# A hybrid SSD / gated-delta / product-key layer on one core: input projections in parts of two, three and three tiles instead of two halves

## The chip, the cores and the metric

One core of a Trainium2 chip runs the whole layer in one launch. The metric is the device time of one execution in microseconds (us), the median of several runs. All data is float32.

## The reference, cut to what matters

```python
def reference(x, ...):                      # x: (1, 1024, 1024)
    for l in range(1):
        x = x + hybrid_mixer(rmsnorm(x, norm_mix_w[l]), w_in[l], ...)
        x = x + peer_ffn(rmsnorm(x, norm_ffn_w[l]), ...)
    return rmsnorm(x, norm_final_w)

def hybrid_mixer(hn, w_in, ...):
    proj = hn @ w_in                        # 1024 -> 3600 columns: z, xBC, dt, qkv, gate, beta, alpha
    xbc = silu(causal_dwconv(proj[xBC], ssd_conv_w) + ssd_conv_b)     # 4 taps along the frames
    qkv = silu(causal_dwconv(proj[qkv], gdn_conv_w))
    ...                                     # SSD scan and gated delta rule, causal from frame to frame
    return concat(y_ssd, y_gdn) @ w_out

def peer_ffn(hn, w_q, sub_keys, u_tab, v_tab):   # per token: 8 heads x 16 experts of 16384
    ...                                          # scores, two top-16, idx and gates (128 per token)
    act = gelu(einsum('td,tkd->tk', hb, u_tab[ib]))
    return einsum('tk,tkd->td', gb * act, v_tab[ib])
```

The input projection is `hn @ w_in`. A convolution over four frames follows it on 20 of its column blocks. The expert part reads 128 rows of `u_tab` and 128 rows of `v_tab` for each token, 4 KB a row.

## The kernel before, in words

The sequence of 1024 frames is cut into 8 tiles of 128. The projection's columns are cut into 29 **units** of 128 columns (the last has 16): units 0 to 19 go through the convolution, 20 to 27 are gates, 28 is the small one of the heads. A unit of some tiles is 8 matmuls that accumulate (one for each 128 rows of `w_in`; the trace shows each as two instructions), then the convolution on VectorE, SiLU on ScalarE, transposes on TensorE, a copy on ScalarE, and stores to scratch tensors in HBM (`tok_scr`, `zgs_scr` by frame, `ch_scr` by channel).

The program has these stages, in order:

- `front_stage` normalises and turns the x tiles (`rms`, `scale_x`, `turn_x`, `weigh`) and projects the **first half**, tiles 0 to 3, so each matmul has 512 columns. Tiles 4 to 7 are normalised between the units (`norm_after`) and kept in SBUF, in slots of the ring that the gathers use later. The order on TensorE is `project(u)`, `turn(u - 1)`, and where `norm_after(u)` names a tile, `turn_x`.
- `tile_stage` first loads constants, then runs `body(0, None)`: the mixer and the product-key selection (`steps`) of tile 0, with the folding of `w_q` and the keys between its pieces. This is "tile 0" below.
- Then come ten **gather stages** e = 0 to 9. Stage e runs `steps` of tile e + 1, the U gathers and dots of tile e (VectorE: 128 gathers of 128 rows, 512 KB each), and the V gathers and sums of tile e - 1 (TensorE: 128 gathers, in pairs). `steps` calls `share()` between its pieces. Each engine then does the items of a list (`SEQUENCES`) that fall to that share, in the list's order: U is a U gather's dot, V a V gather's sum. Every engine works in its own program order, so an item whose input is late holds up all that stands behind it there.
- The **second half** of the projection, tiles 4 to 7 in units of 512 columns, is in stage e = 0: items B (matmuls), Q (copy out of PSUM), K (convolution), Z (SiLU), D (transposes), Y (copy). `first_sequence` places them by shares: D and Y of the unit before, then B, Q, K of this one, then Z. There is one buffer for the copy out of PSUM (`b_pre`) and one for the sums (`b_mixed`). SP loads the weights of unit u + 2 behind the stores of unit u.

The gathers go through a ring of slots of 512 KB, in turn. POOL issues a gather when the slot's last user is done. In stage 0 the ring has `FEW` = 6 slots, because the other 5 hold the turned tiles and a unit's weights; from stage 1 on it has all 11. The weights of a unit are read from `w_in` as it lies, 128 columns wide, so in rows of 512 bytes.

## Time and profile before

| | |
|---|---|
| median of 3 runs | 3464.66 us (3463.91 to 3464.87) |
| the profiled execution | 3463.27 us |
| its span, first to last instruction | 3461.5 us |
| so around the span | 1.8 us |
| TensorE busy, mean granted clock | 2560.1 us (74%), 0.903 |
| VectorE busy | 2069.9 us (60%) |
| ScalarE busy | 469.0 us (14%) |
| GpSimd busy (it issues the gathers) | 1983.2 us (57%) |
| moved by DMA | 1167.46 MB, 337 GB/s over the span |

Busy shares are averages over stages with different limits, so the table only says that no engine is full all the time. What limits a stage has to be read stage by stage. A granted clock of 1.0 is TensorE's level of 2.4 GHz, 0.5 that of 1.2 GHz; a value between is a mixture over the stretch.

### The profile page before, as it was taken

How to read it: one execution, taken by the hardware profiler on the slowest of the kernel's cores; microseconds unless marked ns; L12 is line 12 of the kernel's file. 1: busy time of each engine (PE TensorE's matmuls, PEld its weight loads, DVE VectorE, ACT ScalarE, POOL GpSimd, SP SyncE). 2: the span in 40 equal slices, each digit the busy share in tenths (PEclk: the TensorE clock that was granted, in tenths of full speed). 3: DMA queues.
4: the chain of work that ended last, by engine and by line, in shares of the span. 5: the costliest groups of instructions: out<-in, count | busy, mean ns of one | idle time of the engine just before them, and what ended most of it. 6: DMA issues, size and time to landing. Idle time of an engine off the chain costs nothing.

```text
span 3461.5 us, 26069 instructions
## 1 busy us (share of the span) xinstructions
PE 2560.1 (74%) x8616; PEld 960.6 (28%) x8616; DVE 2069.9 (60%) x4643; ACT 469.0 (14%) x1001; POOL 1983.2 (57%) x2099
## 2 busy tenths in 40 slices
PE   7996636698578757875787587857885888566698
PEld 3446324443233113311421142113211421111111
DVE  3304365558886758685777577767776776544400
ACT  3314112233211001001010100010001100000000
POOL 1110011123477767776777677767776777777775
PEclk9998867799799989998999899989998989888999
DMA  4444045467899999999999999999999999999998
GB/s 121 131 122 140 0 147 164 146 224 248 318 406 409 409 407 396 410 409 407 397 409 409 406 398 409 409 403 400 409 409 403 402 409 409 410 410 410 409 402 355
DMA packets 395350, 1167.46 MB, mean 337 GB/s; under 512 B 40720, under 2 KB 120368, under 8 KB 395216
## 3 DMA queue, kind: packets, MB, share of 16 engines
q0 software_dynamic: 298112, 1082.93, 79.8%
q1 hardware_dynamic: 94048, 78.52, 7.2%
q10 hardware_dynamic: 3056, 4.35, 0.3%
q8 instruction: 69, 1.13, 0.1%
q14 instruction: 65, 0.53, 0.0%
HBM read 1143.57 MB, written 22.09 MB: 337 GB/s over the span
## 4 chain that ended last, share of the span: by engine, by line
POOL 33%; PE 18%; DMA 17%; issue 12%; DVE 9%; ACT 2%; SPq 0%; DVEq 0%; POOLq 0%; ACTq 0%
POOL ring L819 33%; DMA ring<-in_peer_v_dram,picks_T 9%; DMA ring<-in_peer_u_dram,picks 7%; PE y_psum L849 6%; PE y_psum L894 3%; DVE ring L1269 2%; PE tile_psum L1047 2%; DVE arena L1502 1%; DVE arena L1506 1%; PE tile_psum L970 1%; PE tile_psum L988 1%; PE tile_psum L989 1%; DVE final_row L1262 1%; PE tile_psum L1026 1%; DVE arena L1509 1%
## 5 line engine op out<-in xcount | busy, mean ns | idle before, releaser
L894 PE MATMUL y_psum<-ring,spread 128*32 128x512 f32 x4096 | 1370.4, 646 | 504.9 <-DMA ring<-in_peer_v_dram,picks_T 503.5
L1269 DVE CUSTOM_DVE_ANT_0 ring<-ring,h_psum 128x1024 f32<-128x1024 f32 x1024 | 1235.7, 1218 | 700.7 <-DMA ring<-in_peer_u_dram,picks 684.5
L819 POOL DMA_INDIRECT ring<-in_peer_u_dram,picks x1024 | 976.0, 953 | 876.5 <-DVE dots L1269 358.4
L819 POOL DMA_INDIRECT ring<-in_peer_v_dram,picks_T x1024 | 970.8, 948 | 360.3 <-issue 284.8
L894 PEld LDWEIGHTS y_psum<-ring,spread 128*32 128x32 f32 x4096 | 265.3, 113 | 1511.0 <-DMA ring<-in_peer_v_dram,picks_T 919.4
L1047 PE MATMUL tile_psum<-w_q,arena 128*128 128x512 f32 x512 | 224.1, 597 | 2.2 <-ACT arena L1214 2.2
L370 PE MATMUL proj<-hn_first,w_blk 128*128 128x512 f32 x448 | 201.5, 605 | 1.3 <-DVE hn_first L474 1.3
L1117 ACT COPY spread<-zero 128x8 f32<-128x8 f32 (+1 forms) x104 | 21.6, 207 | 1080.0 <-PE y_psum L894 1080.0
L1047 PEld LDWEIGHTS tile_psum<-w_q,arena 128*128 128x128 f32 x512 | 97.3, 191 | 127.6 <-issue 124.8
L1026 PE MATMUL tile_psum<-w_out,arena 128*128 128x512 f32 x256 | 118.0, 605 | 0.0
L1297 DVE SCALAR_TENSOR_TENSOR res<-res,stat_e,final_row 128x1024 f32<-128x1024 f32 x8 | 10.3, 1283 | 177.3 <-ACT stat_e L1134 177.3
L370 PEld LDWEIGHTS proj<-hn_first,w_blk 128*128 128x128 f32 x448 | 85.3, 195 | 100.0 <-issue 98.3
L849 PE MATMUL y_psum<-ring,res 128*128 128x512 f32 x224 | 108.1, 639 | 5.4 <-DMA res<-in_w_in_dram 5.4
L849 PE MATMUL y_psum<-ring 128*128 128x512 f32 x224 | 108.7, 642 | 3.1 <-DMA ring<-in_w_in_dram 3.1
L1259 DVE TENSOR_SCALAR final_row<-b_pre,taps 128x512 f32<-128x512 f32 x20 | 9.7, 486 | 149.8 <-ACT b_pre L1082 149.8
L988 PE MATMUL tile_psum<-arena 128*128 128x128 f32 x320 | 71.0, 306 | 31.4 <-ACT arena L1172 21.6
L346 POOL DMA_DIRECT2D tok_scr<-frames x18 | 13.6, 755 | 125.5 <-ACT frames L441 125.5
L1269 DVE DVE_READ_ACCUMULATOR2_ANT dots<- 128x1 f32 x1024 | 84.2, 82 | 0.0
L989 PE MATMUL tile_psum<-arena 128*128 128x128 f32 x384 | 76.1, 292 | 5.4 <-ACT arena L1172 5.4
L970 PE MATMUL tile_psum<-arena 128*128 128x128 f32 x384 | 58.4, 298 | 27.4 <-DVE arena L1423 27.4
L970 PEld LDWEIGHTS tile_psum<-arena 128*128 128x128 f32 x384 | 49.8, 202 | 59.9 <-issue 59.5
L1026 PEld LDWEIGHTS tile_psum<-w_out,arena 128*128 128x128 f32 x256 | 46.7, 191 | 68.4 <-issue 64.2
(234 smaller groups left out, 2239.8 us busy)
## 6 DMA issues: line engine op xcount, KB each, us to landing
ring<-in_peer_u_dram,picks POOLq DMA_INDIRECT x1024, 8.4
ring<-in_peer_v_dram,picks_T POOLq DMA_INDIRECT x1024, 9.8
w_blk<-in_w_in_dram SPq DMA_DIRECT2D x28, 512.0 KB, 3.8
ring<-in_w_q_T_dram SPq DMA_DIRECT2D x16, 512.0 KB, 3.7
ring<-in_w_in_dram SPq DMA_DIRECT2D x14, 512.0 KB, 7.8
res<-in_w_in_dram SPq DMA_DIRECT2D x14, 512.0 KB, 7.8
arena<-tok_scr SPq DMA_DIRECT2D x8, 768.0 KB, 9.1
tok_scr<-frames POOLq DMA_DIRECT2D x18, 256.0 KB, 2.9
```

The source lines that it names most:

```text
L370: last = nc.tensor.matmul(proj[u % 2][0:width(u)], w, hn[0][:, k], start=(k == 0), stop=(k == KD - 1))
L819: pool.indirect_dma_start(ring[:, j], None, tables[kind], bass.IndirectOffsetOnAxis(ap=at, axis=0)).then_inc(filled[j], 16)
L849: last = nc.tensor.matmul(y_ps[0:unit_width(n), n % 2], w, hn[:, k], start=(k == 0), stop=(k == KD - 1))
L894: last = nc.tensor.matmul(y_ps[quad * STEPS:(quad + 1) * STEPS, half], lines[:, quad, at:at + STEPS], ring[:, j, half * BANK:(half + 1) * ...
L970: last = nc.tensor.matmul(heads(1)[:, h], M_T[:, n % 2, h], X[:, h], start=True, stop=True)
L988: nc.tensor.matmul(heads(2)[:, h], Y[:, h], MX[:, h], start=True, stop=True)
L989: last = nc.tensor.matmul(heads(0)[:, h], MX[:, h], Y[:, h], start=True, stop=True)
L1026: last = nc.tensor.matmul(bank[:, 1 + half], mixT[:, k], w_out[:, k, half * BANK:(half + 1) * BANK], start=(k == 0), stop=(k == KD - 1))
L1047: last = nc.tensor.matmul(bank[:, SCORE_BANKS[b]], h_T[:, k], w_q[:, k, b * BANK:(b + 1) * BANK], start=(k == 0), stop=(k == KD - 1))
L1262: stt(out=b_mixed, in0=b_pre[:, tap:tap + HALF], scalar=taps[:, tap, n:n + 1], in1=b_mixed, op0=ALU.mult, op1=ALU.add).then_inc(s["b_tap"], 1)
L1269: nc.vector.tensor_tensor_reduce(out=ring[:, j], in0=ring[:, j], in1=h_ps[:], scale=1.0, scalar=0.0, op0=ALU.mult, op1=ALU.add, accum_out= ...
L1502: tt(chosen, rank_ps[:, None, None, :].broadcast_to(full), top_rank[:, hs, :, None].broadcast_to(full), ALU.is_equal).then_inc(s["chosen_r ...
```

## The change

The projections now come in three parts:

- **Tiles 0 and 1** in `front_stage`, 256 columns a matmul. Six tiles (2 to 7) are normalised between the units, one in every third. The convolution reads the matmul's result straight from PSUM, so `pre` and its copy go. Four weight buffers stand in place of two. The turned tiles 5 to 7 are written to a new scratch tensor `hn_scr`. The constants of `tile_stage` are loaded here too.
- **Tiles 2 to 4** in gather stage 0, 384 columns a matmul. The items are placed by gathers (`with_units`): B and Q, K and Z two gathers later, D and Y three more gathers later. There are two buffers for the sums, the convolution reads PSUM, its first tap is taken on ScalarE as it copies, and SP loads the next weights ahead of the stores.
- **Tiles 5 to 7** in gather stages 1 to 3, 9, 10 and 10 units, 384 columns each, in the PSUM bank that the transposes use too (`b_bank`), with one weight buffer and one sums buffer.

The ring has `FEW` = 7 slots in stages 0 to 3, and 11 from stage 4 on. The weights are laid out by units on the host (`w_units`), so that a partition reads 4 KB in one piece. They are read three times instead of twice.

The diff, cut to its core:

```diff
-HALF = SEQ // 2
-HALF_TILES = HALF // P
+FIRST_TILES, PART_TILES = 2, 3
+PARTS = 1 + (TILES - FIRST_TILES) // PART_TILES
+FIRST, PART = FIRST_TILES * P, PART_TILES * P
+LATE = (PARTS - 1) * UNITS
+UNITS_OF = {0: (0, UNITS)} | {1 + n: (UNITS + UNITS * n // 3, UNITS + UNITS * (n + 1) // 3) for n in range(3)}
-FEW = 6
+FEW = 7
+def with_units(seq, ends, e):
+    first, to = UNITS_OF[e]
+    total = len([item for item in seq if item[0] in "UV"])
+    begin, gap = (1, 2) if e == 0 else (16, 5)
+    points = []
+    for n in range(first, to):
+        at = begin + (total - begin - 3 * gap) * (n - first) // (to - first)
+        points += [(at, n, "BQ"), (at + gap, n, "KZ"), (at + 2 * gap + (e == 0), n, "DY")]
...
+FEW_STAGES = max(UNITS_OF) + 1
 for e, items in enumerate(GATHERS):
+    if e == FEW_STAGES:
+        CYCLE, count = [*range(FEW, SLOTS), *((count + j) % FEW for j in range(FEW))], 0
     for n, item in enumerate(items):
-        j = n % FEW if e == 0 else CYCLE[later % SLOTS]
-        later += e > 0
+        j = count % FEW if e < FEW_STAGES else CYCLE[count % SLOTS]
...
             def load_w(u):
-                if u >= 2:
-                    sp.wait_ge(proj_done, u - 1)
-                sp.dma_start(w_blk[:, u % 2], w_in[:, :, col:col + P]).then_inc(w_loaded[u % 2], 16)
+                if u >= W_BUFS:
+                    sp.wait_ge(proj_done, u - W_BUFS + 1)
+                    sp.dma_start(w_blk[:, u % W_BUFS], A["w_units"][u]).then_inc(w_loaded[u % W_BUFS], 16)
...
             def norm_after(u):
-            return HALF_TILES + u // 4 if u % 4 == 1 and u < 4 * HALF_TILES else None
+            return FIRST_TILES + u // 3 if u % 3 == 1 and u < 3 * (TILES - FIRST_TILES) else None
...
             def conv(u):
-                dve.wait_ge(pre_done, u + 1)
+                dve.wait_ge(proj_done, u + 1)
+                nc.vector.tensor_copy(halo[:, u], proj[u % 2][:, FIRST:])
...
                 if e == 1:
+                    all_stored(UNITS)
...
+                for n in range(*UNITS_OF.get(e, (0, 0))):
+                    if n < UNITS - 2 or n >= UNITS - 1:
+                        load_unit(n + 2 if n < UNITS - 2 else n + 1)
+                    tile, u = FIRST_TILES + n // UNITS * PART_TILES, n % UNITS
+                    if by_channel(u):
+                        sp.wait_ge(s["b_silu"], n + 1)
+                        sp.dma_start(ch_scr[u, :, tile * P:tile * P + PART], unit_sums(n)).then_inc(b_ch_stored[n % 2], 16)
+                    if by_token(u):
+                        sp.wait_ge(s["b_framed"], LATE_TURNED[n] + 1)
+                        sp.dma_start(part["frames_out"](tile, PART_TILES, u), ...)
...
-                    if e == 1 and j >= FEW and turn_of(item, e) == 1:
-                        pool.wait_ge(s["b_proj"], UNITS)
+                    if j >= FEW and turn_of(item, e) == 1:
+                        pool.wait_ge(s["b_proj"], LATE)
...
                 if kind == "Q":
+                        nc.scalar.copy(unit_bank(n)[:, 0:HALO], halo[:, u]).then_inc(s["b_pre"], 1)
+                        nc.scalar.copy(halo[:, u], unit_bank(n)[:, PART:PART + HALO])
+                        nc.scalar.activation(unit_sums(n), unit_bank(n)[:, 0:PART], ACT.Copy, scale=taps[:, 0, u:u + 1]).then_inc(s["b_pre"], 1)
```

On TensorE, at the head of the front stage (`proj` is a unit's result, `turned` its transposes, `x_turned` an x tile), before and after:

```order
L358 MATMUL x_turned<-ident_f,x_in 128x128 x32
L370 MATMUL proj<-hn_first,w_blk 128x512 x16
L381 MATMUL turned<-ident_f,conv_sum 128x128 x4
L358 MATMUL x_turned<-ident_f,x_in 128x128 x8
L370 MATMUL proj<-hn_first,w_blk 128x512 x8
```

```order
L400 MATMUL x_turned<-ident,x_in 128x128 x16
L408 MATMUL proj<-hn_first,w_blk 128x256 x16
L419 MATMUL turned<-ident,conv_sum 128x128 x2
L400 MATMUL x_turned<-ident,x_in 128x128 x8
L408 MATMUL proj<-hn_first,w_blk 128x256 x8
```

Two x tiles stand ahead of the first unit instead of four, and each unit is half as wide; a turned x tile still stands behind the second unit.

On TensorE in gather stage 0, around the scores of tile 1 (`y_psum<-ring` is a unit's matmuls, `b_turned` or `b_bank` its transposes, `tile_psum` a piece of `steps`), before and after:

```order
L857 MATMUL b_turned<-ident_m,final_row 128x128 x4
L849 MATMUL y_psum<-ring 128x512 x8
L857 MATMUL b_turned<-ident_m,final_row 128x128 x4
L849 MATMUL y_psum<-ring,res 128x512 x8
L951 MATMUL tile_psum<-arena 128x64 x8
L956 MATMUL tile_psum<-ident_m,arena 128x128 x4
L962 MATMUL tile_psum<-S_ssd,arena 128x256 x2
L857 MATMUL b_turned<-ident_m,final_row 128x128 x4
```

```order
L901 MATMUL y_psum<-ring,res 128x384 x8
L909 MATMUL b_bank<-ident,final_row 128x128 x3
L1003 MATMUL tile_psum<-arena 128x64 x8
L901 MATMUL y_psum<-ring 128x384 x8
L909 MATMUL b_bank<-ident,final_row 128x128 x3
L1008 MATMUL tile_psum<-ident,arena 128x128 x4
L1014 MATMUL tile_psum<-S_ssd,arena 128x256 x2
L1022 MATMUL tile_psum<-arena 128x128 x4
```

The transposes now stand behind the next unit's matmuls, not ahead of them, and the units are spread by gathers.

On TensorE at the start of gather stage 1 (`y_psum<-ring,spread` is a pair of V gathers), before and after:

```order
L866 MATMUL y_psum<-y,ident_m 128x512 x2
L916 MATMUL tile_psum<-arena 128x128 x2
L894 MATMUL y_psum<-ring,spread 32x512 x4
L920 MATMUL tile_psum<-rate,upper 128x12
L921 MATMUL tile_psum<-rate,ones 128x12
```

```order
L918 MATMUL y_psum<-y,ident 128x512 x2
L901 MATMUL b_bank<-ring 128x384 x8
L968 MATMUL tile_psum<-arena 128x128 x2
L946 MATMUL y_psum<-ring,spread 32x512 x4
L972 MATMUL tile_psum<-rate,upper 128x12
L973 MATMUL tile_psum<-rate,upper 128x12
```

A unit's matmuls now stand between the V gathers and the pieces of `steps` here, and at 28 more places in stages 1 to 3.

## Rows read from the trace of the kernel before

**Rows 1.** Busy times by stage: front, tile 0, gather stages 0, 1 and 2.

```profile
core 0: us, PE busy (x) PEld busy (x) DVE busy (x) ACT busy (x) POOL busy (x), PEclk, DMA share, GB/s
25.40:260.50 235.10, 222.26 (x604) 103.88 (x604) 62.01 (x88) 71.43 (x125) 26.46 (x37) 0.98 0.40 121
260.50:457.00 196.50, 113.05 (x627) 84.59 (x628) 93.60 (x309) 55.78 (x168) 0.00 (x0) 0.80 0.19 62
457.00:919.20 462.20, 339.86 (x949) 177.83 (x947) 287.76 (x636) 142.74 (x194) 123.57 (x132) 0.84 0.63 205
919.20:1267.00 347.80, 255.83 (x907) 88.93 (x907) 247.19 (x565) 29.98 (x74) 253.43 (x266) 0.91 1.03 407
1267.00:1605.00 338.00, 252.59 (x892) 85.89 (x893) 241.10 (x554) 27.79 (x70) 241.87 (x255) 0.91 1.02 405
```

**Rows 2.** Timeline of TensorE, front stage (start, us, instruction): tile, two units, last transposes.

```profile
45.02 1.81 PE L358 MATMUL x_turned<-ident_f,x_in 128*128 128x128 f32 x8 [2.14 <-DVE x_in L469]
...
232.05 7.03 PE L370 MATMUL proj<-hn_first,w_blk 128*128 128x512 f32 x16
...
239.35 7.03 PE L370 MATMUL proj<-hn_first,w_blk 128*128 128x512 f32 x16
...
253.72 1.20 PE L381 MATMUL turned<-ident_f,conv_sum 128*128 128x128 f32 x8
```

**Rows 3.** Timeline of TensorE in tile 0: four instructions of 256 columns.

```profile
301.97 1.03 PE L962 MATMUL tile_psum<-S_ssd,arena 128*128 128x256 f32 x4
```

**Rows 4.** Timeline of ScalarE and GpSimd, front stage: SiLU, norm's end, bias load.

```profile
39.29 0.72 ACT L453 ACTIVATE conv_sum<-conv_sum,conv_bias 128x512 f32<-128x512 f32 x1 [1.49 <-DVE conv_sum L484]
...
43.98 0.20 ACT L413 ACTIVATE rstd<-log_ms 128x1 f32<-128x1 f32 x1
...
21.24 0.88 POOL L337 DMA_DIRECT2D conv_bias<-in_ssd_conv_b_dram  x1
```

**Rows 5.** Groups by form, VectorE: multiply-add of 512 and 128 columns, scaling a tile.

```profile
L1262 DVE SCALAR_TENSOR_TENSOR final_row<-b_pre,taps,final_row 128x512 f32<-128x512 f32 x60 | 45.1, 751 | 2.1
L1362 DVE SCALAR_TENSOR_TENSOR arena<-tile_psum,logs,floor 128x128 f32<-128x128 f32 x96 | 25.6, 342 | 9.4 <-PE tile_psum L907 9.4
L469 DVE TENSOR_SCALAR x_in<-x_in,rstd 128x1024 f32<-128x1024 f32 x8 | 6.1, 756 | 34.0 <-ACT rstd L413 28.8 <-DMA ident_f<-in_c_ident_dram 5.3
```

**Rows 6.** Timeline of SP at `tile_stage`'s start: first constant, first load of tile 0.

```profile
260.55 0.34 SPq L750 DMA_DIRECT2D ident_m<-in_c_ident_dram  x1
...
264.33 0.52 SPq L760 DMA_DIRECT2D arena<-tok_scr  x1
```

**Rows 7.** Chain of waits over 457 to 925 us: shares by line, two pieces.

```profile
by line: PE y_psum L849 43.0%; DVE final_row L1262 6.5%; PE tile_psum L1047 5.9%; DMA res<-in_w_in_dram 4.9%; issue 4.6%; DMA ring<-in_w_in_dram 3.9%; PE b_turned L857 3.6%; PE tile_psum L1026 2.9%; PE tile_psum L988 2.2%; PE tile_psum L989
...
459.07 18.43 DMA ring<-in_w_in_dram
...
843.68 11.88 DMA res<-in_w_in_dram
```

**Rows 8.** Waits over gather stage 0: who, for whom, total us, times, longest.

```profile
DVE final_row L1259 <- ACT b_pre L1082: 149.8, 20, 12.3
```

**Rows 9.** DMA queues of the page: packets, MB, share of 16 engines.

```profile
q1 hardware_dynamic: 94048, 78.52, 7.2%
```

**Rows 10.** The gathers' issues (L819) over 919 to 1945 us.

```profile
  DVE dots L1269: 34.7, 31
  PE y_psum L894: 34.1, 37
...
DMA to landing us min/median/max: 5.4/8.7/16.5
```

**Rows 11.** Stretches of 20 us in stage 2 (columns of rows 1); a V pair.

```profile
1347.00:1367.00 20.00, 15.74 (x90) 9.57 (x90) 15.57 (x27) 2.88 (x7) 15.31 (x16) 0.91 1.03 408
1367.00:1387.00 20.00, 17.96 (x115) 11.18 (x115) 13.26 (x24) 2.56 (x6) 13.81 (x15) 1.00 0.99 373
...
1079.17 1.91 PE L894 MATMUL y_psum<-ring,spread 128*32 128x512 f32 x8
```

More of the change, by code:

```diff
@@ L441, in frame @@
                     nc.scalar.copy(frames[:, u % 2, :, 0:width(u)], turned[u % 2][:, :, 0:width(u)]).then_inc(frames_done, 1)
[L443 removed]
+            for i in range(FIRST_TILES):
                 rms(i)
@@ L521, with tile_stage @@
 ARENA = 11024
-def tile_stage(nc, A, half, ch_scr, tok_scr, zgs_scr, out, w_out, w_q, ring, w_late_loaded):
+def tile_stage(nc, A, part, fixed, ch_scr, tok_scr, zgs_scr, hn_scr, out, w_out, w_q, ring, w_late_loaded, consts_loaded):
     ctx, sb, ps, sem = scope(nc)
@@ L562, in tile_stage @@
         res = sb("res", [P, D])
[L563 removed]
         final_row = sb("final_row", [P, D])
[L565 to L568 removed]
+        b_late = sb("b_late", [P, PART])
+        b_w = [ring[:, SLOTS - 1], res[:]]
+        hn, taps, conv_bias, halo = (part[n] for n in ("hn", "taps", "bias", "halo"))
         picks_T = [sb(f"picks_T{j}", [P, P], U32) for j in range(2)]
@@ L920, in steps @@
                 nc.tensor.matmul(bank[:, 0, 0:HEADS], upper[:], rate[:], start=True, stop=True)
-                nc.tensor.matmul(bank[:, 0, HEADS:2 * HEADS], ones[:], rate[:], start=True, stop=True).then_inc(s["cums_ready"], 1)
+                nc.tensor.matmul(bank[:, 0, HEADS:2 * HEADS], ones, rate[:], start=True, stop=True).then_inc(s["cums_ready"], 1)
                 share()
@@ L1102, in do @@
+                if kind == "Y" and by_token(n % UNITS):
+                    act.wait_ge(s["b_turned"], LATE_TURNED[n] + 1)
+                    if by_channel(n % UNITS):
+                        act.wait_ge(b_ch_stored[n % 2], 16 * len([k for k in range(n % 2, n + 1, 2) if by_channel(k % UNITS)]))
+                    nc.scalar.copy(unit_frames(n)[:, :, 0:unit_width(n)], b_turned[:, :, 0:unit_width(n)]).then_inc(s["b_framed"], 1)
                 if kind == "G":
```

422 lines of the change are left out of this document (213 added, 209 removed).

## The prediction

> **What bounds the kernel now.** I read the busy times by stage first, because an average over this kernel hides four different limits [rows 1]. In the front stage TensorE is busy 222 of 235 us while the DMA share is 0.40, so the width and number of matmuls set it. Tile 0 takes 196.5 us and is a chain of small steps. Gather stage 0 takes 462.2 us with TensorE at 340, VectorE at 288 and DMA at 0.63: no engine and no queue is full, so a chain through several engines sets it. From stage 1 on the DMA share is 1.02 to 1.03 at 405 to 407 GB/s, with TensorE busy 253 and VectorE 241 of 338 us. Those stages are bound by the gathers' bytes, 256 gathers in 338 us, 1.32 us each.
>
> The chain of waits over stage 0 says what its chain is made of [rows 7]: 43.0% of 468 us, about 200, is the units' matmuls, 8.8% or 41 us is waiting for unit weights (18.4 of it at the start, 11.9 and 10.9 near the end), 6.5% or 30 us the convolution's multiply-adds, 3.6% or 17 us the transposes. The whole width of a unit is on the path. The waits agree: VectorE stood 149.8 us at the head of 20 convolutions, 7.5 us each, for the copy that follows the unit's matmuls [rows 8], with the dots and the steps of tile 1 queued behind it.
>
> So the change takes work out of two stages where it is on the path, and puts a third of it into three stages where DMA is full and TensorE has some 85 us free.
>
> **The front stage.** A unit with its transposes takes 7.30 us (239.35 - 232.05) [rows 2]. With 256 columns both parts halve: 3.65 us. Four instructions of 256 columns take 1.03 us [rows 3], so 16 of them take no more than 4.1 us; I take 3.65 and keep 4.3 as the upper bound of a unit.
>
> Six tiles are now normalised between units. Such a tile is ready after this sequence: convolution of the unit before, about 1.9 us (three multiply-adds of 256 columns at 0.48, between the 0.34 of 128 and the 0.75 of 512 columns [rows 5], and 0.5 for the first tap and the halo, an estimate from the same rows), SiLU 0.45 (half of 0.72, plus some), 4.2 us from SiLU's end to the end of `rstd` (40.0 to 44.2) [rows 4], and 0.76 for the scaling [rows 5]. That is 7.3 us, of which the next unit covers 3.65. With the hand-overs TensorE then idles about 4 us (2.1 before) [rows 2], and turns the tile in 1.8 us. Three units with one tile: 3 x 3.65 + 1.8 + 4 = 16.8 us, and six of these are 101 us. The first convolution cannot start before the bias lands, issued at 21.2 [rows 4], so at about 26. Then 26 + 101 + 10 x 3.65 + the tail of 6.8 us (253.7 to 260.55) [rows 2, 6] = 170 us against 260.5: **-90 us**. With units of 4.3 us it is -71; if the idle time shrinks by half it is -102. The weights are loaded four units ahead, and half of the old DMA share was unused, so the loads, the constants that move in and the 1.6 MB for `hn_scr` are hidden. If they weren't, each unit would wait for 0.5 MB, and that is the -71 case again.
>
> **Setup.** Eight constant loads on SP stand ahead of the first load of tile 0, 260.55 to 264.33 [rows 6]. They go: **-4 us**. Tile 0 stays.
>
> **Gather stage 0.** Matmuls: 200 us x 384/512 = 150, **-50**. Transposes: three for four, **-4**. Weight waits: the two late ones of 11.9 and 10.9 us come from a load that stands behind the unit's stores on SP; now it stands ahead of them, **-22**. The start (18.4 us) stays, since it shares the queues with the loads of tile 1. The copy and convolution: VectorE now does two dots before it turns to K, the first tap is on ScalarE, and TensorE does the next unit before D. Of the 7.5 us wait for each convolution about 2.6 are filled and 1.7 go with the narrower unit (counted already); the multiply-adds fall from 0.75 to about 0.62. What is left on the path I estimate at 1 us less for each of 20 units, **-20**. Sum **-96**, so 366 us. The bounds are -50 (the matmuls alone) and -130 (all of the convolution and transposes hidden). TensorE's own sum, 340 - 54 = 286 us, excludes more. The seventh ring slot gives nothing, since the gathers don't set this stage.
>
> **Gather stages 1 to 3.** Nine or ten units each. Bytes: 9.67 x 0.524 = 5.1 MB of weights, at 405 GB/s 12.5 us. The stores: about 9.3 x 384 + 2.7 x 128 = 3,900 packets. The 94,048 packets of SP's queue took 7.2% of 3461 us [rows 9], 2.65 ns each over all 16 engines, so 10 us. Together 23 us a stage on a full queue, with nothing to hide it. One 1.6 MB load of the turned tiles adds 4 us once.
>
> TensorE: 16 instructions of 384 columns and three transposes, 5.5 us a unit, 53 us a stage on top of 253. That fits in 361 us on average, but not evenly: between 1367 and 1387 us TensorE was busy 18 of 20 us and the gathers' rate fell to 373 GB/s [rows 11]. The ring is 7 slots for 11 there. At 1.32 us each, 11 slots give a gather 14.5 us from its issue until its slot is free, 7 give 9.2. It needs 5.4 us to land at best (8.7 in the median, in a longer queue [rows 10]) and 1.9 us for a V pair [rows 11], 7.3 in all. About 2 us are left, where now POOL hardly waits for a slot (69 us in three stages) [rows 10]. A V pair that finds a unit of 5.1 us ahead of it uses more than that. I take 1.2 us lost for each unit, **12 us** a stage; nothing is the lower bound, all of TensorE's 53 us the upper. So a stage takes 35 us more, **+105** for three, between +54 (half of the 23 hidden behind the present gaps, and the start) and +228.
>
> **The sum.** 3463.3 (the profiled execution; the median of the runs is 3464.7, 1.4 more) - 90 - 4 - 96 + 4 + 105 = **3382 us**.
>
> **Rivals.**
> *The late units nearly free.* The ring of 7 is enough and the stores slip between gathers: +54 for +105, 3331 us. For it: 2 us of slack for each gather, and TensorE idle for a quarter of the stage. Against it: the DMA share is above 1.0, so bytes can't be free.
> *The late units cost their whole width: slower.* In stages 1 to 3 each unit blocks the V pairs, the seven slots fill, POOL stops and the queue runs dry, so a unit costs its 5.5 us of TensorE beside its bytes: 76 us a stage, +228, 3505 us. It decides against the change from 62 us a stage on, where three stages eat up 186. For it: stage 0, where just so 43% of the path is units; the stretch at 1367 us. Against it: most stretches of stage 2 kept 408 GB/s at 15 to 20 us of TensorE work.
> *Stage 0 shrinks by its matmuls alone,* since the steps of tile 1 are the chain and fill what the convolutions leave: -50 for -96, 3428 us. For it: tile 0 alone takes 196 us for such a chain, and 128 dots come on top.
> *Narrow matmuls don't shrink as their width,* since a weight load stands before each. The four instructions of 256 columns took 1.03 us [rows 3], 0.26 each where the half of the present ones is 0.21: at most 29 x 16 x 0.05 = 23 us lost in the front, 3405 us. Against it: the 0.26 holds the last one's drain. The Trainium skill (TensorE: Matmul & The Clock Gate, The mechanism) says that a weight load overlaps a running matmul only when their row groups differ, and gives a load of 128 columns 0.107 us, which would make it an estimated 50 us and 3432. By that rule 512 columns would show it too, and the trace disagrees: 7.03 us for 16, which leaves nothing between them [rows 2].
>
> **How the numbers follow.** A difference under 0.2% (7 us) can't be told from no change here. Chances: the forecast's case 0.47, late units nearly free 0.20, stage 0 by matmuls alone 0.12, narrow matmuls 0.02, late units at their whole width 0.15, and 0.04 for a sum of these that lands within 7 us. So faster 0.81, same 0.04, slower 0.15. The range of 8 in 10 reaches from 3315 (late units nearly free, and a little more from stage 0) to 3475 (stage 0 by its matmuls alone and stages 1 to 3 at 50 us more each, or those at 65 by themselves), leaving out the slower case's far half.
>
> **What would show it.** The start of tile 0's loads near 170 us; units of 3.65 us in the front with gaps of about 4 us ahead of each turned tile; stage 0 (first gather to the last dots) near 366 us, with no wait over 5 us for unit weights after its start; stages 1 to 3 near 375 us with a DMA share still close to 1.0, and from stage 4 on 338 to 340 as now. If stages 1 to 3 show POOL waiting for slots for more than 50 us each at a DMA share under 0.95, the ring's price was taken too low. If stage 0 is above 410 us, its chain wasn't the units'. Either would make the prediction wrong.

## The result, and the profile after

The changed kernel takes 3431.0 us in the median of four runs (3426.8 to 3437.1), beside 3464.8 (3463.9 to 3465.2) for the kernel before. The ratio is 0.9905, 95% interval 0.9891 to 0.9919: 34 us less, a gain clear of the 0.2% that counts, and inside the forecast range, where the forecast was 81 us less. The profiled execution is the slowest of the four, 3437.1 us with a span of 3435.3, so the trace has 26 us to explain and not 34. All ratios are of undisturbed executions; one of the kernel before, beside some of the experiments, took 5267.7 us and is left out.

Busy times by stage of the changed kernel: front, tile 0, gather stages 0 to 4. From stage 1 on a stage is cut here from the last U dot of one stage to the last of the next.

```profile
core 0: us, PE busy (x) PEld busy (x) DVE busy (x) ACT busy (x) POOL busy (x), PEclk, DMA share, GB/s
25.00:175.00 150.00, 119.48 (x540) 100.76 (x538) 51.42 (x112) 55.72 (x99) 23.73 (x36) 0.89 0.51 169
178.80:368.80 190.00, 112.76 (x627) 84.56 (x628) 93.38 (x308) 55.67 (x168) 0.00 (x0) 0.81 0.17 60
368.80:731.80 363.00, 262.39 (x922) 159.88 (x920) 269.38 (x615) 137.66 (x212) 123.95 (x131) 0.86 0.76 260
731.80:1118.30 386.50, 296.75 (x1027) 117.20 (x1027) 256.99 (x582) 64.69 (x128) 236.28 (x251) 0.89 0.97 364
1118.30:1510.30 392.00, 304.43 (x1084) 118.01 (x1084) 260.71 (x586) 72.81 (x142) 242.86 (x257) 0.92 0.98 372
1510.30:1897.90 387.60, 302.67 (x1084) 117.06 (x1084) 245.22 (x561) 63.11 (x114) 243.82 (x256) 0.93 0.97 370
1897.90:2239.70 341.80, 251.94 (x894) 87.42 (x894) 242.68 (x557) 29.01 (x72) 244.70 (x258) 0.92 1.02 405
```

Cut at the same points, the kernel before has 329.2, 340.2, 339.2 and 340.2 us in stages 1 to 4, the first two of them these:

```profile
918.60:1247.80 329.20, 243.05 (x862) 85.08 (x862) 241.21 (x557) 26.48 (x67) 240.31 (x253) 0.91 1.03 408
1247.80:1588.00 340.20, 253.37 (x894) 86.12 (x894) 242.94 (x558) 29.02 (x72) 244.41 (x258) 0.91 1.02 405
```

Stages 1 to 3 pay 57.3, 51.8 and 48.4 us more, 157.5 together. From the end of stage 3 on the two profiles differ by 3 us in all.

The other mark is the cast of the picks, which ends a tile and releases the gathers of its stage. Timeline of VectorE, the casts ahead of and behind stage 0, first before, then after:

```profile
456.95 0.22 DVE L1301 CAST picks<-arena 128x128 uint32<-128x128 f32 x1
914.97 0.22 DVE L1301 CAST picks<-arena 128x128 uint32<-128x128 f32 x1
```

```profile
368.80 0.22 DVE L1351 CAST picks<-arena 128x128 uint32<-128x128 f32 x1
728.14 0.22 DVE L1351 CAST picks<-arena 128x128 uint32<-128x128 f32 x1
```

The first cast comes 88.2 us earlier. Stage 0, cast to cast, falls from 458.0 to 359.3 us, by 98.7. So -88.2 - 98.7 + 157.5 + 3 = -26 us, the difference of the two profiled executions.

Front stage, timeline of TensorE with the transposes of a normalised tile, and of SP with the first load of tile 0:

```profile
100.20 3.62 PE L408 MATMUL proj<-hn_first,w_blk 128*128 128x256 f32 x16
...
107.85 1.97 PE L400 MATMUL x_turned<-ident,x_in 128*128 128x128 f32 x8 [3.81 <-DVE x_in L499]
109.61 4.12 PE L408 MATMUL proj<-hn_first,w_blk 128*128 128x256 f32 x16
```

```profile
178.85 0.33 SPq L797 DMA_DIRECT2D arena<-tok_scr  x1
```

The unit behind a turned tile takes 4.12 us here, and up to 5.71, where the others take 3.62. TensorE idles before each turned tile, and the granted clock is lower in the unit behind it. Windows over one unit each, behind the fifth and the sixth turned tile, then one with no tile ahead:

```profile
109.61:113.73 4.12, 4.12 (x19) 3.54 (x19) 1.43 (x2) 0.51 (x1) 0.00 (x0) 0.88 0.02 6
126.87:132.58 5.71, 5.71 (x19) 4.63 (x19) 1.43 (x2) 0.51 (x1) 0.00 (x0) 0.63 0.01 1
136.31:139.93 3.62, 3.62 (x20) 3.16 (x19) 2.00 (x5) 0.88 (x2) 0.71 (x1) 1.00 0.78 283
```

Stage 0, the waits: who, for whom, in all, times, longest; then the chain of waits over the stage, shares by line.

```profile
DVE final_row L1312 <- ACT final_row L1144: 67.0, 14, 9.4
...
PE y_psum L901 <- DMA ring<-in_w_units_dram: 24.4, 3, 19.8
...
PE y_psum L901 <- DMA res<-in_w_units_dram: 5.8, 4, 3.5
```

```profile
by line: PE y_psum L901 23.4%; DVE ring L1319 21.4%; PE tile_psum L1099 7.5%; DVE final_row L1312 5.7%; DMA ring<-in_w_units_dram 5.3%; PE tile_psum L1078 4.6%; DVE arena L1559 2.8%; issue 2.0%; DVE arena L1552 1.9%; DVE arena L1556 1.9%; D
```

The units' matmuls were 43.0% of the chain [rows 7] and are 23.4%; the dots (L1319), not among its first ten lines before, are 21.4%. The convolution's wait of 149.8 us [rows 8] is 67.0. TensorE idles 30 us for unit weights, 19.8 of it in the first wait. That is more than before. The waits of TensorE for unit weights in the old stage 0:

```profile
PE y_psum L849 <- DMA res<-in_w_in_dram: 5.4, 2, 3.5
PE y_psum L849 <- DMA ring<-in_w_in_dram: 3.1, 3, 1.4
```

Stages 1 to 3, the gathers' issues on GpSimd: what ended POOL's idle time (us, times), and the time from issue to landing.

```profile
  PE y_psum L946: 202.3, 126
  issue: 170.9, 556
  DVE dots L1319: 70.1, 81
...
DMA to landing us min/median/max: 4.2/6.4/11.3
```

POOL waits 272 us for a free slot in three stages, where it waited 69 [rows 10]. The landing is shorter than before, 6.4 for 8.7 us. (Both traces give the landing of only some nine in ten of these gathers.) That doesn't look like a queue with more bytes to carry; it looks like one with less in it.

### The profile page after: what moved, and what is told of

It is laid out like the page before. It is cut to its first block, busy times and chain, and to the rows that moved or that the text cites. A ratio compares the mean times of both kernels' runs of the same rounds, so it can differ in the third digit from the quotient of the medians.

```text
span 3435.3 us, 27404 instructions
## 1 busy us (share of the span) xinstructions
PE 2539.3 (74%) x9080; PEld 1040.8 (30%) x9080; DVE 2073.3 (60%) x4704; ACT 561.3 (16%) x1160; POOL 1975.4 (58%) x2097
## 4 chain that ended last, share of the span: by engine, by line
POOL 24%; DMA 24%; PE 22%; DVE 13%; issue 10%; ACT 2%; SPq 0%; DVEq 0%; ACTq 0%; POOLq 0%
POOL ring L869 24%; DMA ring<-in_peer_v_dram,picks_T 14%; DMA ring<-in_peer_u_dram,picks 9%; PE y_psum L946 7%; DVE ring L1319 4%; PE b_bank L901 3%; PE y_psum L901 2%; PE tile_psum L1099 2%; PE tile_psum L1078 2%; DVE arena L1552 1%; DVE arena L1556 1%; PE tile_psum L1040 1%; DVE arena L1559 1%; PE tile_psum L1041 1%; PE tile_psum L1022 1%
## 5 line engine op out<-in xcount | busy, mean ns | idle before, releaser
L1319 DVE CUSTOM_DVE_ANT_0 ring<-ring,h_psum 128x1024 f32<-128x1024 f32 x1024 | 1236.3, 1218 | 809.2 <-DMA ring<-in_peer_u_dram,picks 795.1
L901 PE MATMUL b_bank<-ring 128*128 128x384 f32 (+1 forms) x464 | 156.0, 490 | 0.0
L1347 DVE SCALAR_TENSOR_TENSOR res<-res,stat_e,final_row 128x1024 f32<-128x1024 f32 x8 | 10.3, 1283 | 176.7 <-ACT stat_e L1195 176.7
L408 PE MATMUL proj<-hn_first,w_blk 128*128 128x256 f32 (+1 forms) x464 | 114.9, 406 | 1.3 <-DVE hn_first L504 1.3
L901 PEld LDWEIGHTS b_bank<-ring 128*128 128x128 f32 (+1 forms) x464 | 85.5, 187 | 75.3 <-issue 23.3
L901 PE MATMUL y_psum<-ring 128*128 128x384 f32 (+1 forms) x240 | 86.3, 516 | 26.0 <-DMA ring<-in_w_units_dram 24.4
L408 PEld LDWEIGHTS proj<-hn_first,w_blk 128*128 128x128 f32 (+1 forms) x464 | 92.5, 205 | 16.7 <-DVE hn_first L504 1.7
L1040 PE MATMUL tile_psum<-arena 128*128 128x128 f32 x320 | 69.2, 300 | 29.6 <-ACT arena L1233 21.6
L901 PE MATMUL y_psum<-ring,res 128*128 128x384 f32 x224 | 81.2, 520 | 5.8 <-DMA res<-in_w_units_dram 5.8
L1319 DVE DVE_READ_ACCUMULATOR2_ANT dots<- 128x1 f32 x1024 | 84.4, 82 | 0.0
L1041 PE MATMUL tile_psum<-arena 128*128 128x128 f32 x384 | 75.1, 290 | 6.3 <-ACT arena L1233 6.3
L1312 DVE SCALAR_TENSOR_TENSOR final_row<-y_psum,taps,final_row 128x384 f32<-128x384 f32 x60 | 37.0, 617 | 68.4 <-ACT final_row L1144 67.0
L1022 PE MATMUL tile_psum<-arena 128*128 128x128 f32 x384 | 54.2, 284 | 17.5 <-DVE arena L1473 17.5
```

Of the source, the lines that this page charges most:

```text
L408: last = nc.tensor.matmul(proj[u % 2][0:width(u), HALO:], weights(u)[:, k], hn[0][:, k], start=(k == 0), stop=(k == KD - 1))
L901: last = nc.tensor.matmul(unit_bank(n)[0:unit_width(n), HALO:HALO + PART], unit_weights(n)[:, k], hn[:, k], start=(k == 0), stop=(k == KD ...
L1022: last = nc.tensor.matmul(heads(1)[:, h], M_T[:, n % 2, h], X[:, h], start=True, stop=True)
L1040: nc.tensor.matmul(heads(2)[:, h], Y[:, h], MX[:, h], start=True, stop=True)
L1041: last = nc.tensor.matmul(heads(0)[:, h], MX[:, h], Y[:, h], start=True, stop=True)
L1312: stt(out=unit_sums(n), in0=unit_bank(n)[:, tap:tap + PART], scalar=taps[:, tap, u:u + 1], in1=unit_sums(n), op0=ALU.mult, op1=ALU.add).th ...
```

## The experiments

Three theories of the 157.5 us: **(A)** the ring of 7 slots by itself, **(B)** the bytes and packets of weights and stores, **(C)** the units' width on TensorE, with V pairs queued behind it. All kernels are edits of the changed one. "Stages 1 to 3" is the sum of the three in the profiled execution; the changed kernel has 1166.1 us, the kernel before 1008.6. Five of the traces have the same stages 1 to 3, that of the changed kernel and of the four below that differ from it in stage 0 alone, and their sums are 1160.6 to 1170.8 us. So a sum is good to some 5 us either way, and every ratio and median below stands beside it. In the diffs `...` marks what is left out.

### The ring without the units

```diff
-LATE = (PARTS - 1) * UNITS
+LATE = UNITS
...
-UNITS_OF = {0: (0, UNITS)} | {1 + n: (UNITS + UNITS * n // 3, UNITS + UNITS * (n + 1) // 3) for n in range(3)}
+UNITS_OF = {0: (0, UNITS)}
...
-FEW_STAGES = max(UNITS_OF) + 1
+FEW_STAGES = 4
...
+                    src = m if m < FIRST_TILES + PART_TILES else m - PART_TILES
...
+                    sp.dma_start(zgs, rows(zgs_scr, src)).then_inc(s["mix_loaded"], 16)
```

With 7 slots:

> Takes the third part's 29 units out of stages 1 to 3 (no weights, no matmuls, no stores; tiles 5 to 7 read the projections of tiles 2 to 4 instead), and keeps the ring at 7 slots up to the end of stage 3. After stood at 3431 us, and stages 1 to 3 paid 158 us more than before for the third part. Theory A (seven slots are too few for a gather's landing and hold, whoever else is there): more than half of the 158 stays, 3350 us or more. Theory B (bytes and packets of weights and stores on a full queue) and theory C (the units' 5.5 us of TensorE ahead of the V pairs, which needs few slots AND units): almost all goes, 3270 to 3290 us, within 10 us of the kernel with 11 slots.

With 11 slots from stage 1 on (the line of `FEW_STAGES` stays):

> The third part's units are left out as in the kernel with 7 slots, and the ring has 11 slots from stage 1 on. All theories: stages 1 to 3 are back at 329 to 340 us each, so 3431 - 158 = 3273 us, in a range of 3260 to 3290. Above 3300 would mean that part of the 158 us is no price of the units or of the ring at all.

Measured: 3346.5 us with 7 slots (ratio to before 0.9666, 0.9650 to 0.9682) and 3281.5 with 11 (0.9477, 0.9462 to 0.9493). Stages 1 to 3 are 1078.5 and 1010.3 us. So the changed kernel's 1166.1 holds 155.8 us for the third part, and **68 of them are the ring** (65 by the medians of the runs), with no unit in these stages. The two kernels differ in the number of slots alone. That is less than half, so A as stated falls, but B and C fall harder: both said under 10. Stage 2 of each kernel, windows:

```profile
1081.50:1446.00 364.50, 259.94 (x894) 88.94 (x894) 242.89 (x558) 29.02 (x72) 242.66 (x257) 0.91 0.99 378
```

```profile
1060.30:1401.50 341.20, 249.36 (x894) 86.33 (x894) 243.08 (x556) 29.01 (x72) 244.07 (x258) 0.93 1.02 404
```

The same bytes (364.5 x 378 = 341.2 x 404 = 138 MB) and the same work, 23 us apart. POOL's waits in stages 1 to 3, with 7 slots and with 11:

```profile
  issue: 181.6, 591
  PE y_psum L947: 118.1, 121
  DVE dots L1320: 55.1, 50
...
DMA to landing us min/median/max: 4.3/6.3/10.2
```

```profile
  issue: 214.2, 701
  DVE dots L1320: 37.6, 33
  PE y_psum L947: 32.0, 30
...
DMA to landing us min/median/max: 5.0/8.9/15.7
```

I matched each gather of the trace with its landing and with the dot or V pair that frees its slot. In stages 1 to 3 of the kernel with 7 slots a slot is in use for 8.6 us on average: 6.4 until landing, then 1.7 (U) or 2.7 (V) until free. On average 6.0 slots of 7 are in use. I put the missing one down to the fixed order in which slots are taken; no run takes them in another, so that isn't shown. The quotient 8.6 / 6.0 = 1.42 us is the time between gathers by the definition of these averages, so it checks the matching and explains nothing by itself.

### The units' pieces, one by one

One of eight matmuls, then 8 of 1024 columns of weights, then one row of 128 of the stores. Each diff is cut to its core, and where stores are left out tiles 5 to 7 read the projections of tiles 2 to 4, as above:

```diff
+                    ks = range(KD) if n < UNITS else range(1)
+                    for k in ks:
```

> Late units make one of their eight matmuls over k (the seven others are left out, so tiles 5 to 7 are computed from an eighth of the sum); weights, stores, transposes, convolutions and slots stay. That takes 7/8 of 5.0 us, 4.4 us of TensorE, from each of 29 units, 127 us in all. Theory C (width): 100 us or more goes, 3330 us or less. Theory B (bytes and packets): within 10 us of 3431. Theory A (slots alone): within 10 us of 3431.

```diff
+                    cols = slice(0, P if n < UNITS else 8)
```

> Late units load 8 of 1024 columns of their weights (the rest of the block is what the slot held before, so tiles 5 to 7 are computed from other weights); matmuls, stores and slots stay, and the load has as many rows as before. That takes 28 x 0.52 = 14.6 MB, at 405 GB/s 36 us, and the 24 us that TensorE waited for these loads. Theory B: 30 to 40 us goes, 3391 to 3401 us. Theory C: at most 10 us goes, since TensorE's width is what the stage pays and the queue has gaps to hide the loads. Theory A: as C.

```diff
+                        rows_n = P if n < UNITS else 1
+                        sp.dma_start(ch_scr[u, 0:rows_n, tile * P:tile * P + PART], unit_sums(n)[0:rows_n]).then_inc(b_ch_stored[n % 2], 16)
```

> Late units store one row of 128 (left out: the rest of the projections of tiles 5 to 7, which read those of tiles 2 to 4 instead); weights, matmuls, transposes, convolutions and the seven slots stay. Of the 156 us that stages 1 to 3 pay over the kernel without late units and with 11 slots, the ring alone showed 68, the eight matmuls 35, the weights 23; the stores are the piece not yet seen. If their packets cost what the prediction took, 10 us a stage: 30 us less, 3401 us. If they slip between gathers: within 10 us of 3431.

Measured: 3401.3 us without the matmuls (0.9825, 0.9809 to 0.9841), 3424.0 without the weights (0.9893, 0.9876 to 0.9909), 3420.6 without the stores (0.9864, 0.9844 to 0.9883). Stages 1 to 3 are 1131.2, 1143.4 and 1158.3 us. Stage 2 of the three in this order:

```profile
1100.60:1484.80 384.20, 278.92 (x944) 98.06 (x944) 259.90 (x586) 72.84 (x143) 243.77 (x257) 0.88 0.99 379
1104.40:1491.20 386.80, 302.87 (x1084) 118.58 (x1084) 259.61 (x588) 72.81 (x142) 242.95 (x257) 0.93 0.96 363
1107.80:1497.80 390.00, 304.20 (x1084) 116.57 (x1084) 260.76 (x586) 72.83 (x142) 243.03 (x257) 0.93 0.97 366
```

C predicted 100 or more for the matmuls and gets 30 to 35. B predicted 36 for the weights and 30 for the stores. It gets 8 to 10 for the stores. For the weights it gets 23 by the stages and 7 by the medians: the profiled execution without them is the fastest of its four and 12 us under their median, so 23 is too high, and by the runs alone the piece isn't told from nothing. With 7 slots and no units the queue draws 378 GB/s where it carries 404 with 11; that much of the units' traffic fits in between is my reading.

All three edits in one kernel:

> Late units with one of eight matmuls, 8 of 1024 columns of weights and one row of 128 of their stores (all left out of tiles 5 to 7, which read tiles 2 to 4); their transposes, convolutions, copies and SiLUs stay, and seven slots. Over 11 slots without units the changed kernel paid 156 us in stages 1 to 3, of which the ring took 68, and leaving out singly gave 35 (matmuls), 23 (weights), 8 (stores). If these add up: 90 us stay, stages 1 to 3 are 1101 us together. If a piece taken alone only showed another one behind it: more goes, down to the ring's 68, 1079 us. If the small steps on VectorE and ScalarE are the real hold-up: 110 us or more stay.

Measured: 3358.6 us (0.9691, 0.9652 to 0.9730), stages 1 to 3 at 1090.3. Stage 2:

```profile
1086.10:1453.40 367.30, 273.08 (x944) 94.52 (x944) 259.18 (x586) 72.84 (x142) 243.75 (x257) 0.91 0.98 375
```

| left out | stages 1 to 3, us less | median of the runs, us less |
|---|---|---|
| matmuls | 35 | 30 |
| weights | 23 | 7 |
| stores | 8 | 10 |
| sum of these | 66 | 47 |
| all three at once | 76 | 72 |

So 72 to 76 us go together, more than the pieces singly: each piece alone hid some of another, 10 us by the stages and 25 by the medians. What stays is 80: the ring's 68 and 12 for what is left of 29 units, above all the copies, convolutions and transposes.

### How many slots

```diff
-        j = count % FEW if e < FEW_STAGES else CYCLE[count % SLOTS]
+        j = count % (FEW if e == 0 else 9) if e < FEW_STAGES else CYCLE[count % SLOTS]
```

The same with 6 in the place of 9; both without late units.

> No late units (left out, tiles 5 to 7 read the projections of tiles 2 to 4), and a ring of 6 slots in stages 1 to 3, where 7 gave 352, 364 and 362 us and 11 gave 330, 341 and 339. A slot of the ring of 7 was in use for 6.4 us of landing and 2.1 us of hold, and 6.0 of the 7 were in use on average: 8.5 / 6.0 = 1.42 us for a gather, as measured. If a ring of N pays (landing + hold) / (N - 1): 6 slots give 8.0 to 8.5 over 5, 1.60 to 1.70 us, 410 to 435 us a stage for stages 2 and 3. If the price of seven slots was something else (a transition, an order of slots): under 385 us.

> No late units, and 9 slots in stages 1 to 3. (Landing + hold) / (N - 1) is 8.5 / 8 = 1.06 us, under the 1.32 us that the full queue gives, so the ring no longer sets the pace: 340 to 345 us for stages 2 and 3. If each missing slot cost alike (5.5 us a stage for each of four): 352.

Measured: 3437.2 us with 6 slots (0.9919, 0.9886 to 0.9951), 3299.2 with 9 (0.9520, 0.9481 to 0.9559). Stage 2, windows, 6 and 9 slots, with the landing of the 6:

```profile
1114.40:1501.90 387.50, 267.14 (x894) 86.77 (x894) 242.86 (x558) 29.02 (x72) 243.03 (x256) 0.91 0.96 356
```

```profile
DMA to landing us min/median/max: 4.1/6.1/10.4
```

```profile
1070.30:1417.20 346.90, 254.09 (x894) 87.96 (x894) 242.94 (x556) 29.02 (x72) 242.65 (x256) 0.91 1.01 397
```

All four kernels without late units; the last two columns are averages over stages 1 to 3, matched as above:

| slots | stage 2, us | GB/s | more than 11 slots, us | slots in use | us that one is in use |
|---|---|---|---|---|---|
| 11 | 341.2 | 404 | 0 | 8.8 | 11.7 |
| 9 | 346.9 | 397 | 6 | 7.6 | 10.3 |
| 7 | 364.5 | 378 | 23 | 6.0 | 8.6 |
| 6 | 387.5 | 356 | 46 | 5.4 | 8.2 |

The forecast for 6 failed: 387.5 us for 410 to 435. A slot is in use for less time as the ring gets shorter, 8.2 us with 6 and not 8.5, and more slots are in use than N - 1, 5.4 and not 5. With 9 and 11 it is fewer than N - 1. So (landing + hold) / (N - 1) is no rule for the price at a depth that wasn't measured. And 9 slots are not free, as I had put it at best: 347 lies between "no longer sets the pace" and "each slot alike", and the three stages together are 23 us longer than with 11. The last slots are cheap and the price of each further one grows.

### Where the units stand

```diff
-        points += [(at, n, "BQ"), (at + gap, n, "KZ"), (at + 2 * gap + (e == 0), n, "DY")]
+        if e == 0:
+            points += [(at, n, "BQ")]
+        else:
+            points += [(at, n, "B"), (at + 1, n, "b"), (at + 2, n, "c"), (at + 3, n, "dQ")]
+        points += [(at + gap, n, "KZ"), (at + 2 * gap + (e == 0), n, "DY")]
```

> The whole computation, with the eight matmuls of a late unit cut into four pairs that stand one gather apart, so that a V pair finds at most 1.3 us of unit ahead of it where it found 5. If the 35 us that came with the leaving out of seven matmuls was V pairs held up in a ring of seven slots: 20 to 35 us less than the changed kernel, 3396 to 3411 us. If it was TensorE's sum that counts (the same work, only cut up): within 10 us of 3431.

```diff
+UNITS_OF = {0: (0, UNITS), 1: (UNITS, 2 * UNITS)}
...
-    begin, gap = (1, 2) if e == 0 else (16, 5)
+    begin, gap = (1, 2) if e == 0 else (16, 3)
```

> All 29 late units stand in stage 1 and the ring has 11 slots from stage 2 on (the steps of one unit stand 3 gathers apart instead of 5). If the seven slots are a price by stage (68 us for three) and the units one by unit (about 3 each): two stages give back 22 to 23 us each, 3386 us. If units close together cost more, up to TensorE's whole 5.5 us each (243 + 160 = 403 us of TensorE in that stage): no gain or a loss, 3431 to 3480 us.

```diff
+UNITS_OF = {0: (0, UNITS)} | {1 + n: (UNITS + UNITS * n // 2, UNITS + UNITS * (n + 1) // 2) for n in range(2)}
```

> The late units stand in stages 1 and 2, and the ring has 11 slots from stage 3 on. Slots priced by stage, units by unit: one stage's 22 to 23 us back, 3409 us. Units close together dearer: 3431 us or more.

Measured: 3422.2 us in quarters (0.9872, 0.9847 to 0.9896), 3421.5 in one stage (0.9876, 0.9856 to 0.9896), 3413.6 in two (0.9845, 0.9826 to 0.9865). The quarters give 9 us (11 by the stages), under what I expected, and their interval overlaps that of the changed kernel: if the V pairs held up by one piece of 5 us cost something, it is the smaller part of the matmuls' 30 to 35. Two stages give 17 for 22 expected. One stage gives 10, not 45. That stage is 469.1 us, 139 over the 329.9 without units; less the ring's 22 it is 4.0 us a unit, where three stages have (156 - 68) / 29 = 3.0 and two have 3.2. Closer units are dearer, and in one stage that eats most of what the ring of two stages gives back. (The steps of a unit stand 3 gathers apart there and not 5, which was not varied by itself.)

Two stages and quarters in one kernel:

> The whole computation: late units in stages 1 and 2 alone (11 slots from stage 3 on, which gave 3414 us where the changed kernel stood at 3431) and their matmuls cut into four pairs, one gather apart (which alone gave 3422). If the two add up: 3404 to 3408 us. If units that stand closer together hold up V pairs more often, and cutting pays more: 3395 to 3403. If close units leave no gathers between which the pairs find room: 3412 or more.

Measured: 3405.3 us (3401.3 to 3409.1), ratio to before 0.9823, 0.9806 to 0.9841. The two add up, within the runs' spread. This kernel computes all that the changed one does and is the fastest of those here that do: 60 us below before (3465.7 beside it, by medians), some 26 below the change.

### Stage 0, its orders and its width

First the loads of unit weights on SP behind the stores again:

```diff
-                    if n < UNITS - 2 or n >= UNITS - 1:
-                        load_unit(n + 2 if n < UNITS - 2 else n + 1)
+                    if n >= UNITS:
+                        load_unit(n + 1)
...
+                    if n < UNITS - 2:
+                        load_unit(n + 2)
```

> In gather stage 0 SP loads the weights of the unit after next behind the stores of a unit again, not ahead of them; all else as in the changed kernel, whose stage 0 is 359.4 us from one cast of picks to the next (four profiled kernels with the same stage 0 agree within 0.1). Theory of the prediction (the two late waits for weights, 22 us, came from that order): stage 0 is 20 us longer, 379 to 382 us, with waits of TensorE for weights over 10 us in it. Rival (four-kilobyte rows load faster, and with a chain that no longer hangs on the units the order doesn't matter): within 3 us of 359.4.

Then the old sequence of a unit's steps:

```diff
+        if e == 0:
+            points += [(at, n - 1, "DY")] if n > first else []
+            points += [(at, n, "BQK"), (at + gap, n, "Z")] + ([(at + 2 * gap, n, "DY")] if n == to - 1 else [])
```

> In stage 0 a unit's steps stand in the sequence as in the kernel before: matmuls, copy and convolution at one place, SiLU two gathers later, transposes just ahead of the next unit's matmuls. Theory of the prediction (the new order took 1 us off the path for each of 20 units): stage 0 is about 20 us longer, 375 to 385 us. Rival (most of the old waiting went with the narrower unit and its smaller sum): within 5 us of 359.4.

Both:

> Stage 0 with both of its new orders undone (a unit's steps in the old sequence, SP's loads behind the stores), so that of the change only the narrower units, the first tap on ScalarE and the rows of four kilobytes are left there. The old stage 0 took 458 us from cast to cast, the new one 359.4. Prediction's terms: 458 - 50 (matmuls) - 4 (transposes) = 404 us, and the two orders 22 and 20 below that. Rival (the two orders hide each other, as each alone put back 54 and 62 us): undoing both costs the longer of the two and little more, 420 to 430 us, so narrowness is worth only 30 to 38. Third (the two add up, 54 + 62): 470 us or more, and narrowness alone is worth nothing.

And the new orders with one of eight matmuls in the units of stage 0:

> The units of stage 0 make one of their eight matmuls over k (the other seven are left out, so tiles 2 to 4 come from an eighth of the sum), 29 x 4.4 = 128 us of TensorE less in that stage. Theory of the prediction (a unit's whole width is on the path of stage 0): the stage falls from 359.4 us by more than 100. Rival (the steps of tile 1 and the dots are the chain by now, and the units fill what they leave): by less than 60, since tile 0 alone took 196.5 us with no dots and no units, and 128 dots of 1.1 us stand beside it.

Measured, with stage 0 from cast to cast beside the run's time:

| kernel | stage 0, us | run, us |
|---|---|---|
| before | 458.0 | 3464.8 |
| changed | 359.3 | 3431.0 |
| loads behind the stores | 413.6 | 3494.6 |
| old sequence of steps | 421.5 | 3495.5 |
| both | 423.7 | 3497.2 |
| one of eight matmuls | 311.5 | 3388.0 |

Each order alone puts back 54 and 62 us, where I expected 20 and the rivals next to nothing. Both together put back 64, as the rival for that run had it: the two don't add, and the change needs the two of them. Undone, either makes the changed kernel slower than before (ratios 1.0085, 1.0062 to 1.0108, and 1.0088, 1.0066 to 1.0109; both undone 1.0096, 1.0065 to 1.0127). The waits of stage 0 with the loads behind, then with both undone:

```profile
DVE final_row L1316 <- ACT final_row L1148: 98.8, 19, 9.8
...
PE y_psum L905 <- DMA ring<-in_w_units_dram: 66.5, 9, 19.4
...
PE y_psum L905 <- DMA res<-in_w_units_dram: 36.3, 6, 8.6
```

```profile
DVE final_row L1320 <- ACT final_row L1152: 140.7, 19, 20.2
...
PE y_psum L909 <- DMA ring<-in_w_units_dram: 18.5, 2, 18.3
...
PE y_psum L909 <- DMA res<-in_w_units_dram: 7.5, 3, 3.7
```

With the loads behind and the new steps, TensorE waits 103 us for weights (30 in the changed kernel). The narrow unit isn't the reason: with both orders undone the units are as narrow and the loads as far behind, and the wait is 26 us. My reading is that the new steps put a unit's transposes, and so its stores, five gathers behind its matmuls, and a load behind those stores then starts too late. That isn't tested by itself. The convolution's wait grows with it, from 67.0 to 98.8. With both undone the convolution's wait is back at 140.7 us, nearly the 149.8 of [rows 8].

Leaving out seven of eight matmuls from stage 0 takes off 48 us (ratio of the run 0.9777, 0.9753 to 0.9802), for 128 us of matmuls by my sum. So less than the whole width is on the path now. Whether all of it was before, no run shows. And 48 understates what the width is worth, because the clock fell with the work. Stage 0 of the changed kernel and of this one:

```profile
368.80:728.10 359.30, 262.39 (x922) 159.88 (x920) 265.70 (x608) 137.66 (x212) 121.39 (x128) 0.86 0.77 261
```

```profile
367.70:679.20 311.50, 148.56 (x516) 94.09 (x514) 265.46 (x609) 137.91 (x212) 121.42 (x128) 0.65 0.86 300
```

The granted clock is 0.65 for 0.86, TensorE is busy 114 us less and not 128, and many small matmuls of the steps of tile 1 take 420 ns in the median where they took 275.

## Why the prediction failed, and where it was right

**Front stage, -90, and setup, -4.** Right: the first load of tile 0 moves from 264.33 [rows 6] to 178.85, -85.5, and tile 0 ran 3 us shorter, -88.2 in all for -94. Units take 3.62 us and the idle time ahead of a turned tile is 3.8 to 4.3, as forecast (3.65 and 4). The miss of 9 us at the first load has three parts. The first convolution is at 27.8 us, not 26. The six groups of three units and a tile take 105 us where I had 101, because the unit behind each turned tile takes 4.1 to 5.7 us at a granted clock of 0.63 to 0.88; over the whole front the clock is 0.89, where it was 0.98 [rows 1]. And eleven units stand behind the groups for my ten.

**Narrow matmuls don't shrink (rival).** False: 16 of 256 columns take 3.62 us against 7.03 of 512 [rows 2], a half. (Half of a present one is 7.03 / 32 = 0.22 us and not 0.21, so the rival's price was 18 us, not 23.)

**Stage 0, -96.** The sum was right, -98.7, and its terms were not; that they meet is luck. The matmuls' -50 and transposes' -4 assume that the whole width stays on the path. What all the rest of the change is worth in this stage with the old orders is 458.0 - 423.7 = 34 us. That is the narrower units, the ScalarE tap and the larger rows, and also the convolution's reading of PSUM, the second sums buffer, the seventh slot and the placing by gathers, which no run takes apart. The two orders, -22 and -20 on my list, are 64 together. The -22 rests on a misreading: the 11.9 and 10.9 us in the chain of waits [rows 7] are the loads' own times, and TensorE idled before those two units for 1.9 and 3.5 us, 8.5 us for weights in all of the stage. There was no late wait of 22 us to remove. With the old steps the loads' order is worth 2 us (423.7 against 421.5), with the new ones 54: it keeps the new steps from making such waits. The -20 priced the dots queued behind the convolution's wait at 1 us a unit. With seven slots in each case, POOL's idle time until a dot frees a slot is 219 us in the new stage 0, 252 with the loads behind, 279 with the old steps and 282 with both undone. So the dots were held up by much more than 1 us a unit. The rival "stage 0 shrinks by its matmuls alone" is false from both sides: narrowness is less than its 50, and it is not alone.

**hn load, +4.** Not measured by itself. Stage 1 paid 57.3 us where its neighbours paid 51.8 and 48.4, which leaves room for about that.

**Stages 1 to 3, +105.** This is the step that failed: 157.5 us were measured. Both halves of it were mis-sized, in opposite directions:
- "Together 23 us a stage on a full queue, with nothing to hide it", 69 us: weights and stores left out singly were 31 by the stages and 17 by the medians. The sentence took the queue to be full as before [rows 1], but the same change takes four slots from the ring, and with 7 the queue is no longer full.
- "The ring is 7 slots for 11", 12 us a stage with the units' matmuls, 36 us: the ring alone is 68, the matmuls 35 more, the small steps 12. The working set what 7 slots allow (9.2 us) against a gather at its best, 5.4 us of landing and 1.9 of a pair. The mean in the run with 7 slots is 6.4 and 2.2, and 6.0 slots are in use at once, not 7: 6.0 x 1.32 = 7.9 us for a need of 8.6. Neither number stood in the trace before. There a slot is in use for 11.5 us on average, and 11.5 / 6.0 would have made a stage 490 us, where 364 were measured, because the landing shrinks as the queue empties. So the trace before gave only bounds, nothing and far too much, and the term was put near the lower one.

The rival "their whole width" gives 76 us a stage and "nearly free" 18; it came to 52.5. The price of a unit, 157.5 / 29 = 5.4 us, happens to equal its 5.5 us of TensorE, but the run with one of eight matmuls shows that this is chance. My marker for the ring's price had two conditions. POOL's waits over 50 us a stage came true (91). A DMA share under 0.95 did not (0.97 to 0.98), because the share was the wrong thing to look at, as below.

Put together: 6 us short in front and tile 0, 3 over in stage 0, 49 short in stages 1 to 3 (157.5 for 105 and hn's 4) and 3 in the later stages make 55, the distance from -81 to -26 between the profiled executions. The change is a gain because the front is shorter by 85 us and stage 0 by 99, 64 of these by its orders. The third part costs in the gather stages about what I estimate for it as 29 wider units in front, three tiles at 1.8 us for each unit [rows 2], 159 us. By that estimate moving that part there was worth nothing by itself; no run has it in front.

## What to carry to other kernels

When a change takes slots from a ring, price the shorter ring by itself, before the bytes that pass through it. A gather's best time against the time that the slots allow is a lower bound, and here it said free where the price was 68 us. The means of the deeper ring don't carry over either, because the landing changes with the depth. One run of the shorter ring without the new work gave the price at once. Terms that remove waits in front of the same queue need not add: undo them one at a time and all together. A transfer in a chain of waits is not idle time of the engine behind it: read the engine's own wait before you count on getting it back. And work that is moved into a stage with a free engine but a short ring isn't hidden there. Here two stages were better than three and than one.

## What the runs showed of the hardware

The DMA share of a stretch is not how full the queue is. With 7 slots it is 0.99 at 378 GB/s and with 11 it is 1.02 at 404, for the same bytes: 0.99 x 364.5 = 361 us of packets' time against 348. At 6 slots it is 0.96 at 356 GB/s. GB/s and the landing tell more: a gather lands in 6.1 to 6.3 us in the median with 6 or 7 slots and in 8.9 with 11 (with 6 slots the trace gives the landing of two gathers in three). So the last slots mostly lengthen the landing, and the rate still rises by 7%. The Trainium skill (Perfetto Trace Analysis, Roofline) bounds a core that is alone at its HBM by its 16 DMA engines, at about 435 GB/s. No stretch here exceeds that, the fullest stretch of 20 us in stage 2 of the kernel before being at 411; and the runs show in addition that the rate reached depends on how many gathers are under way.

TensorE's clock follows what it did before. In the front stage it idles 3.8 to 4.3 us ahead of a turned tile, and the next unit runs at a granted clock of 0.63 to 0.88 and takes 4.1 to 5.7 us for 3.62. In stage 0 with an eighth of the units' matmuls it is 0.65 for 0.86.

What stays open: why all but the orders gives 34 us in stage 0 and not 54 was not taken apart further, what the load of the turned tiles costs was not measured, no run takes the slots in another order, and a ring of 8 slots was not run.
